# A hybrid decoder step: ACT rounds 27 weight tiles of the first block, and the memory stage is put in another order

## The reference

```
h = x + W_out [ HGRN2(hn) || chunk-gMLP(hn) ],  hn = RMSNorm(x) through one input projection W_in
h = h + CrossAttn(RMSNorm(h), K/V of 256 memory tokens)        (4 heads of 256)
h = h + W_down relu(W_up RMSNorm(h))^2,      y = RMSNorm(h)
```

## Time and profile before

| | us |
|---|---|
| median of 3 runs (2953.66 to 2956.56) | 2955.88 |
| the profiled execution | 2955.48 |
| its span, first to last instruction | 2953.7 |
| PE busy | 2889.2 |
| memory stage, to the first matmul of zf | 0 to 142.75 |
| first block to the end of its first 29 tiles | 142.75 to 223.96 |
| head-by-head part of the first block | 223.96 to 344.27 |
| the same part of the second block | 943.40 to 1033.84 |

### The profile page before, as it was taken

How to read it: one execution, slowest core, us unless ns; L and a number is a source line. 1 busy time by engine, 2 the same in 40 slices (tenths; PEclk the granted TensorE clock), 3 DMA queues, 4 the chain that set the end, 5 groups by cost and what they waited for, 6 DMA issues and landing times.

```text
span 2953.7 us, 40414 instructions
## 1 busy us (share of the span) xinstructions
PE 2889.2 (98%) x17203; PEld 2334.5 (79%) x17203; DVE 1273.9 (43%) x2093; ACT 627.6 (21%) x967; POOL 484.3 (16%) x389
## 2 busy tenths in 40 slices
PE   7998899999999999999999999999999999999998
PEld 6786788777888888778888888887778888877787
DVE  5679733444343833322243744222334483322223
ACT  4423221201013411110112422110002341111011
POOL 0197505788830000000000000000000000000000
PEclk9999999999999999999999999999999999999999
DMA  8795657998975455666566455676767545567654
GB/s 289 279 339 199 243 188 248 348 326 282 331 281 185 147 188 193 239 209 214 202 213 238 152 171 182 197 252 229 293 223 286 185 145 192 178 226 280 241 188 152
DMA packets 207676, 675.92 MB, mean 229 GB/s; under 512 B 22864, under 2 KB 28240, under 8 KB 207504
## 3 DMA queue, kind: packets, MB, share of 16 engines
q1 hardware_dynamic: 200480, 662.72, 64.3%
q10 hardware_dynamic: 7024, 10.68, 1.0%
HBM read 542.84 MB, written 130.48 MB: 228 GB/s over the span
## 4 chain that ended last, share of the span: by engine, by line
PE 88%; DVE 10%; ACT 1%; DMA 1%; issue 0%; POOL 0%; ACTq 0%; SPq 0%; DVEq 0%; POOLq 0%
PE half L913 79%; DVE lvl L2149 3%; PE half L921 2%; PE half L1235 2%; DVE lvl L2162 2%; PE half L1047 1%; PE half L930 1%; DVE bn L2218 1%; PE half L1115 1%; PE half L1245 0%; DVE ends L2157 0%; DVE state L2198 0%; DMA w_pairs<-stage 0%; DVE stats L2245 0%; PE half L1103 0%
## 5 line engine op out<-in xcount | busy, mean ns | idle before, releaser
L913 PE MATMUL half<-a_hi,w_ring 128*128 128x512 f32 x2560 | 822.9, 397 | 0.1
L913 PE MATMUL half<-w_ring,a_hi 128*128 128x512 f32 x2176 | 678.1, 393 | 0.0
L913 PE MATMUL half<-w_ring,ht_hi 128*128 128x512 f32 x2016 | 626.6, 392 | 0.0
L913 PEld LDWEIGHTS half<-a_hi,w_ring 128*128 128x128 f32 x2560 | 480.2, 188 | 132.4 <-issue 15.1
L913 PE MATMUL half<-a_lo,w_ring 128*128 128x512 f32 x1280 | 505.4, 395 | 0.0
L913 PEld LDWEIGHTS half<-w_ring,a_hi 128*128 128x128 f32 x2176 | 411.0, 189 | 90.7
L913 PEld LDWEIGHTS half<-w_ring,ht_hi 128*128 128x128 f32 x2016 | 378.9, 188 | 82.5
L913 PE MATMUL half<-w_ring,a_lo 128*128 128x512 f32 x1088 | 434.4, 399 | 3.1 <-DVE a_lo L1778 2.4
L913 PE MATMUL half<-w_ring,ht_lo 128*128 128x512 f32 x1008 | 395.4, 392 | 0.4 <-DVE ht_lo L2368 0.4
L2376 DVE SCALAR_TENSOR_TENSOR x<-half,rstd,x 128x512 f32<-128x512 f32 x252 | 171.8, 745 | 301.1 <-PE half L913 301.1
L844 POOL TENSOR_TENSOR w_ring<-w_raw,zero 128x512 fp32r<-128x512 f32 x192 | 230.3, 1199 | 341.4 <-PE half L930 134.5
(11 more groups left out here) (300 smaller groups left out, 2408.3 us busy)
## 6 DMA issues: line engine op xcount, KB each, us to landing
w_ring<-w_pairs SPq DMA_DIRECT2D x704, 512.0 KB, 3.3
w_pairs<-w_ring SPq DMA_DIRECT2D x192, 512.0 KB, 5.0
w_pairs<-stage SPq DMA_DIRECT2D x16, 1024.0 KB, 4.9
w_raw<-in_w_up SPq DMA_DIRECT2D x64, 256.0 KB, 4.7
w_raw<-in_w_down SPq DMA_DIRECT2D x64, 256.0 KB, 4.0
w_s<-in_w_up SPq DMA_DIRECT2D x8, 2048.0 KB, 11.9
w_s<-in_w_down SPq DMA_DIRECT2D x8, 2048.0 KB, 11.3
w_raw<-in_w_in SPq DMA_DIRECT2D x48, 256.0 KB, 4.0
```

What stands on the lines that cost most here:

```text
L913: m = nc.tensor.matmul(ps[:, j, :], l, r, start=(i == 0 and q == 0), stop=(i == tiles_in - 1 and q == 2))
```

## The change

In the first block, ACT writes the hi parts of tiles 29 to 55 (SBUF to SBUF copies, at fixed places between its own work: `FILLER_HI`), each after waits for the slot's store, for the raw tile and for the slot's last use; POOL waits for them and only subtracts for these tiles. In the first block DVE multiplies `uu` as soon as the mixing is done; the mixing of the first twelve recurrence tiles with rstd and gate, which stood ahead of it in unit 6, comes behind the loop over units. The other blocks keep their order.

```diff
+FILLERS = (29, 56)
+FILLER_HI = {"zq": range(29, 33), "kt": range(33, 34), 0: range(34, 38), 1: range(38, 42), 2: range(42, 45), 3: range(45, 47), 4: range(47, 48),
+             5: range(48, 52), 6: range(52, 56)}
...
+            for i in range(first, after):
+                pool.wait_ge(filler_hi, i - first + 1)
+                nc.gpsimd.tensor_tensor(w_lo[:, i % RING, :], w_raw[:, i % RAW, :], w_hi[:, i % RING, :].bitcast(F32),
+                                        ALU.subtract).then_inc(w_split.sem, 1)
...
+                def filler_tiles(at):
+                    for i in FILLER_HI.get(at, ()) if pos == "first" else ():
+                        act.wait_ge(w_stored[i % RING].sem, i // RING * 16 + 16)
+                        act.wait_ge(w_in[i % RAW].sem, i // RAW * 16 + 16)
+                        act.wait_ge(w_used.sem, W_TILES["mem"] + i + 1)
+                        nc.scalar.copy(w_hi[:, i % RING, :], w_raw[:, i % RAW, :]).then_inc(filler_hi, 1)
...
                 decays(1)
+                filler_tiles("zq")
                 act.wait_ge(*done(pos, "kt"))
                 nc.scalar.copy(kdt[:], rows_of(out_of(pos, "kt"), 3)).then_inc(evacuated_of(pos, "kt"), 1)
+                filler_tiles("kt")
...
                     if u == 5:
                         rsqrt(pos, "oa", 12)
+                    filler_tiles(u)
...
                     if u == 6:
-                        refine(pos, "oa", 12)
-                        for t in range(3):
-                            mixed(t)
+                        if pos != "first":
+                            mixed_rows()
...
+                if pos == "first":
+                    mixed_rows()
                 dve.wait_ge(o_ready.sem, o_ready.at(pos, UNITS - 1))
```

```diff
-ROWS_AT = {3: 1, 6: 0}
+ROWS_AT = {4: 1, 6: 0}
+STORES = (6, 6, 2, 2)
+WARM = 20
...
+            for i in range(WARM):
+                nc.tensor.matmul(half[1][:, 3, 0:P], zero[:].to_broadcast([P, P]), zero[:].to_broadcast([P, P]),
+                                 start=True, stop=True)
...
+            gemm(pos, ("ck", 0), "M", a_hi, a_lo, MT, needs=[("nm", MT - 1)])
+            query_weight(0)
+            gemm(pos, ("ck", 1), "M", a_hi, a_lo, MT)
+            pe.wait_ge(*step("xn1"))
+            to_columns("n1", half[1][:, 3, :], tiles_of(xns0))
...
+            gemm(pos, ("cv", 0), "M", a_hi, a_lo, MT)
+            gemm(pos, ("cv", 1), "M", a_hi, a_lo, MT, turns=range(4))
+            rows_to_features(("cvt", 0), [("cv", 0)])
+            gemm(pos, ("cv", 1), "M", a_hi, a_lo, MT, turns=range(4, 8))
...
-            mean_squares(pos, "nm", MT, [x[:, 1, :]], [xn[:, 1, :]])
             for t in range(MT):
-                scaled_row("nm", t, xn[:, t, :], x[:, t, :])
-            split_lo(0)
+                nc.vector.tensor_tensor(xn[:, t, :], x[:, t, :], gain[:], ALU.mult).then_inc(xn_ready.sem, 1)
...
+            features_hi("cvt", 0, vt_hi)
+            n1_squares(pos, 1)
+            split_hi(9)
             rows_out("cv", 1)
...
             for j in range(KD):
                 store_folded(("nv", j))
+                if j in (5, 6):
+                    load("first", j - 1, I["w_in"][0], 0, 512, range(j - 1, j))
```

More of the change, by code:

```diff
@@ L304, in program @@
         with ExitStack() as z:
+            with ExitStack() as y:
+                stage += [sb(f"stage{i}", [P, 2, 2, 512], F32R, y) for i in (2, 3)]
             kt_hi = sb("kt_hi", [P, KD, NM], F32R, z)
@@ L691, in block_loads @@
                     if i == 0 and pos == "first":
-                        load(pos, 4, w_in_, 0, c, range(4, 8))
+                        load(pos, 6, w_in_, 0, c, range(6, 8))
                     else:
@@ L851, in _ @@
                 pool.sem_inc(w_stored[s].sem, 16)
-            with pool.Fori(0, FOLD0 // RING) as g:
+            first, after = FILLERS
+            with pool.Fori(0, first // RING) as g:
                 for k in range(RING):
@@ L956, in _ @@
                 transposes(pos, ("nm", t), [xn[:, t, k * P:k * P + P] for k in range(KD)])
-            for c in range(2):
-                gemm(pos, ("ck", c), "M", a_hi, a_lo, MT, needs=[("nm", MT - 1)])
             def rows_to_features(job, needs):
@@ L967, in query_weight @@
                 transposes(pos, ("wq", k), [wq[:, k % 4, i * P:i * P + P] for i in range(KD)],
-                           back=1 if k == 0 else 2, bank0=2 * (k % 2))
+                           back=2, bank0=first_bank(("wq", k)))
             def key_product(k):
-                begin(pos, ("mq", k), needs=[("wq", k)], back=1 if k == 0 else 2)
+                begin(pos, ("mq", k), needs=[("wq", k)], back=2)
                 ps = folded_banks(pos, ("mq", k))
                 for h in range(H):
+                    if k == 0 and h % 2 == 0:
+                        pe.wait_ge(*out(pos, ("ckt", h // 2)))
                     for i in (2 * h, 2 * h + 1):
@@ L984, in value_product @@
                 pe.wait_ge(mem_lo.sem, mem_lo.at(pos, 8 + h))
-                begin(pos, ("nv", j), needs=[("cvt", 1)], back=1 if j == 0 else 2)
+                begin(pos, ("nv", j), needs=[("cvt", j // 4)], back=1 if j == 0 else 2)
                 ps = folded_banks(pos, ("nv", j))
@@ L1893, in _ @@
             norm_s("n1", "xn1", xs0[:], xns0[:], gain[SQ, :], (ss, var, y0, yt, rstd))
-            for c in range(2):
-                features_lo("ckt", c, kt_hi, kt_lo)
             dve.wait_ge(lb_exps, 1)
@@ L1917, in _ @@
             split_lo(8)
+            features_lo("cvt", 0, vt_hi, vt_lo)
+            n1_statistics(pos, 1)
             dve.wait_ge(ws_transposed, 1)
@@ L1920, in _ @@
                                     masks[:, 7:8, :].to_broadcast([P, H, P]), ALU.mult).then_inc(setup_ready, 1)
-            for c in range(2):
-                features_lo("cvt", c, vt_hi, vt_lo)
+            n1_row_scaled(1, 0)
             split_lo(9)
-            n1_rows_scaled(pos, 1)
             for j in range(KD):
@@ L1928, in _ @@
                 staged_lo(("nv", j))
+                if j == 0:
+                    n1_row_scaled(1, 1)
+                if j == 1:
+                    features_lo("cvt", 1, vt_hi, vt_lo)
                 if j in (1, 3):
@@ L2209, in mixed, with mixed_rows @@
                     ins.then_inc(mixed_ready.sem, 1)
+                def mixed_rows():
+                    refine(pos, "oa", 12)
+                    for t in range(3):
+                        mixed(t)
                 dve.wait_ge(*out(pos, "zf"))
```

145 lines of the change are left out of this document (92 added, 53 removed).

## The result

The changed kernel takes 2935.93 us (median of 5 runs, 2933.21 to 2942.22) against 2955.88 us before: a ratio of 0.9939, 95% interval 0.9928 to 0.9950, so 20 us or 0.6% faster. The forecast was 2930 us, the range 2913 to 2949. The profiled execution took 2933.21 us (span 2931.4), 22.3 us under the profiled execution before; the sum of the prediction said 25 for it. The median lies 2.7 us above it, and the runs are spread more widely than before (9 us instead of 3).

A forecast was written before the change was run, and what follows sets the result against it. PE, busy for 2889.2 of 2953.7 us, was taken to bound the kernel. The head-by-head part's 14 us and the memory stage's 11 us make 25: 2955.5 - 25 = 2930.5, rounded 2930 us; range 2913 to 2949.

The forecast's parts named there:

- The part: Head-by-head part of the first block, transposes of ends to those of vv: 120.3 to about 106 us, 14 us less.
- The price of a POOL instruction: Head-by-head part: each POOL instruction running beside DVE adds 0.78 us to DVE's total.
- The rule weighed in the prediction: A two-SBUF-input DVE instruction and an SBUF-reading GpSimd one exclude each other; subtractions cost DVE as much apiece as roundings.
- The memory stage: From 11.65 to 142.75 us before the change: the block starts 11 us sooner, bounds 0 to 21.
- 29.9 us; nothing moves that: Start: weight group 3 lands at 29.9 us, 10.4 us after issue; keys end at 39.9 instead of 41.4 us.
- The folding: Memory stage: DVE's half splits remove 3.6 us of waiting for wt_lo; waits for stores give back 2 us.
- rival D: Memory stage is paced by its transfers and starts the block no sooner: 2941 us; chance 0.10.
- The values: Memory stage: splitting cvt removes 2.9 us (vt_lo) and slow clock; ACT's cv 1 behind row 2's squares costs about 3 us.
- B: Head-by-head part: DVE stays saturated in units 1 to 3, the 29.9 us stay; 2944 us; chance 0.13.
- E: Neither head-by-head part nor memory stage gains: no change, 2955 us; chance 0.06.
- A: Head-by-head part runs like the second block but for 2.7 us at oto; memory stage saves 14; about 2917 us; chance 0.20.
- C: Slower: DVE's streams keep POOL out, 7.0 us per burst, 35 us by tile 51; 2965 us; chance 0.05.

The follow-up runs named there:

- the eight profiles: Profiled kernels sharing the changed kernel's memory stage, zeros and order of loads unchanged; block starts between 133.85 and 136.74 us, 134.8 in the mean.
- the kernel with the memory stage alone: Changed kernel's memory stage kept, but POOL rounds all tiles and the mixing stands inside unit 6, as before the change; 2951.03 us, ratio 0.9985.

## Why the prediction was right, and where its steps were not

*The part* was forecast at 14 us less and about 106 us, and measured at 14.0 and 106.30; its excess over the second block is 15.9 us, the number of the sum. Its terms held nearly as well. The first wait of 4.4 us for lvl is gone: four subtractions fall ahead of the part, 23 into it. PE's waits in units 1 to 3 are 7.3 us (7.5 forecast), and with 18 of the subtractions left out they vanish, which shows that they are POOL's doing. uu is 3.7 us late (3 forecast): ACT is idle for 3.9 us before its roundings of tiles 48 to 51, of which the first begins at 294.28 us, and gelu follows 86.4 us after the part's start where 84.5 was forecast (ACT's last rounding and gelu):

```profile
299.79 0.62 ACT L1673 CAST w_ring<-w_raw 128x512 fp32r<-128x512 f32 x1 [1.24 <-DMA w_raw<-in_w_out]
...
301.73 1.88 ACT L1708 ACTIVATE uu<-half 128x2048 f32<-128x2048 f32 x1
```

The wait at vv is 1.9 us (2.7 forecast). These three make 12.9 us of the 13.2 forecast, of which the second block has 0.7 as well. The slow clock, put at 2.7 us, shows in PE's busy time, 3.7 us over the second block's (92.0 and 88.3), with two half-rate stretches of 3.4 us in the part (from 238.63 and 303.48 us). That the sum was met to 0.1 us is luck: its terms were off by 0.2 to 1.0 us, to both sides.

The price of a POOL instruction was right only as a mean. The 18 subtractions left out cost DVE 0.77 us apiece (0.78 forecast), but all 23 only (90.48 - 75.96) / 23 = 0.63 us, and the 24 roundings and one subtraction that went out of the part (113.30 - 90.48) / 25 = 0.91 us. So DVE was busy for 90.5 us and not for 94. The rule weighed in the prediction (the Trainium skill, SBUF — State Buffer, Who interferes with whom) made a subtraction as dear for DVE as a rounding. By the runs a subtraction does hold DVE up, but what stayed cost less apiece than what went; whether that is the kind of instruction or the place where it falls was not told apart.

One number on the way was off without harm: POOL ended tile 28 at 204.8 us, 10.5 us ahead of the part and not 20. It never ran eight tiles ahead, since it waited 4.7 us for tiles 4 and 5 and then took 2.4 us for a tile, 2.6 in the end, which is little less than PE's 2.8.

*The memory stage* was mis-sized: 11 us forecast, 8.4 measured (8.0 in the mean of the eight profiles). Of its edits only the products of zeros were taken out by themselves, so how the gain divides among the others is read from the traces and not shown. By stages:

- To the first folded product: 5.4 us forecast (2.4 for the start, 3 for kt_lo and the slow clock), 3.7 measured (49.40 to 45.71 us; 3.2 in the mean). The step that failed is the start, "29.9 us; nothing moves that", which was to end the keys at 39.9 us. They end at 41.5 us, as late as before, with one query transpose (0.9 us) done by then, so 0.8 us came of the 2.4. PE's next work behind the keys:

```profile
41.44 0.68 PE L979 MATMUL half<-ident,xns 32*128 32x32 f32 x8
```

  Group 3 landed at 31.4 us, 12.2 us after its issue, and PE stood for it. The 10.4 us that were taken are the median of three loads; this one took 10.8 us in the kernel before. Loaded ahead of the query weights it lands in 8.4 us. The 3 us behind the keys did come, 2.9 without the query transpose. And the products of zeros, taken as worth 0, were worth 0 when taken away: they save 1.5 us in the transposes, and PE stands for group 3 instead.
- The folding: 1.6 us less forecast (3.6 for wt_lo, 2 given back to the stores), 1.3 us more measured (34.00 to 35.30 us; 34.0, so nothing gained, in the mean). The halves did shrink the two waits for wt_lo from 3.6 to 1.4 us. But the sum gave back too little: a third one of 2.3 us and a wait of 1.1 us for wq took their place. ACT waits 6.31 us for a stage buffer, and what PE needs next is queued behind it (ACT, then DVE, then PE, then SP's store that ACT waited for, KB and us to landing):

```profile
66.02 1.02 ACT L1461 ACTIVATE wt_hi<-half 128x1024 fp32r<-128x1024 f32 x1
73.35 1.02 ACT L1461 ACTIVATE stage<-half 128x1024 fp32r<-128x1024 f32 x1 [6.31 <-DMA w_pairs<-stage]
74.27 1.02 ACT L1461 ACTIVATE wt_hi<-half 128x1024 fp32r<-128x1024 f32 x1
```

```profile
75.55 1.22 DVE L1839 TENSOR_TENSOR wt_lo<-half,wt_hi 128x1024 fp32r<-128x1024 f32 x1
```

```profile
76.82 0.38 PE L963 MATMUL half<-kt_hi,wt_lo 128*128 128x256 f32 x1 [2.26 <-DVE wt_lo L1839]
```

```profile
w_pairs<-stage SPq DMA_DIRECT2D x1, 1024.0 KB, 9.9
```

  With the value groups out of that store's way the folding took 5 us less than here, and 2.8 less than in the shortest of the eight profiles. So rival D was true of one part of the stage: transfers pace the folding, and not the whole.
- The values: 4.0 us forecast (the 8.6 less the two terms above, 3 and 1.6), 6.0 measured (59.35 to 53.36 us; 4.7 in the mean). With four stage buffers ACT has no wait for a store here, and the squares of row 2 cost PE 2.5 us around cvt 1 (0.6 for kn and 1.9 for the low half of the first folded value, L963 on stage; 3 forecast).

Of the rivals, B and with it E fell (the part did gain), A fell (the subtractions are not hidden), and C fell: POOL was not kept out, its 27 subtractions behind ACT's roundings take 1.38 us in the mean. Two numbers of A don't come out of the rows: its "94 of 103 us" (its own part is 90.4 + 2.7, some 93 us, which DVE's 94 us would not fit into), and its sum, which takes the 2.7 us at oto in twice (29.9 - 2.7 is the 27 already; 2914 us without it).

## What to carry to other kernels

An engine that keeps order passes a wait on: before a store's wait is called short, look at what stands behind it in the same queue and what shares its transfers. A reordering is priced only for the wait that is last at the time: uu ahead of the mixing costs 1.5 us while gelu is late and saves 3.4 us when it isn't, by the traces. A bulk load moved out of one way must be followed to the next tile behind it. And a clock of 1.00 is no reading where the clock has no record: the time of one product tells.

## What the runs showed of the hardware that was not expected

Products of zeros ahead of the first work gave PE full clock for the first transposes (2.18 instead of 3.65 us), but with the pause of 3.6 us behind them PE was at half rate for 3.4 or 6.8 us of the stretch from 13 to 21 us in eight of nine profiles. Without the zeros (one profile) it was at half rate up to 21.4 us, first transposes and first key products alike. With the pause filled (two profiles) it was at full rate from the transposes on. The ninth, the one with the value groups later, was at full rate with the pause too, so it doesn't hang on the pause alone.

In four of the profiles PE stood still for 1.3 to 1.8 us in the midst of the same row of products in the last block, with nothing that the trace names to wait for; the longest, of the kernel with the memory stage alone:

```profile
2379.85 0.43 PE L1086 MATMUL half<-lvl 128*32 128x16 f32 x16 [1.81 <-issue]
```

A half-rate stretch of 3.4 us follows in three of them. This is one of the places where runs of one kernel differ; its cause is open.
